# Index logits of a sparse attention: the matmuls of two heads issued in turn, lower and upper rows, into two sets of banks

## The chip, the cores and the metric

The kernel runs on one core of one Trainium2 chip. The metric is the device time of one execution in microseconds; below it is the median of three executions. The profile is of one further execution.

## What is computed

Two residual blocks run over one sequence of 512 tokens with 1024 channels. The second ends in a layer whose sparse attention first scores every key for every query. With 8 index heads of 64 channels, for a block of 128 queries:

```python
logits = jnp.einsum('bqhd,bkd->bqhk', qi, k_idx_f)
score = jnp.einsum('bqh,bqhk->bqk', wi, jax.nn.relu(logits))
score = jnp.where(s_pos[None, None, :] <= t_pos[None, :, None], score, -jnp.inf)
_, idx = lax.top_k(score, topk)
```

`qi` are 8 heads of queries, `k_idx_f` one set of keys for all heads, `wi` one weight per token and head. All three come out of one projection of the normed input (`idx_in` in the kernel). The keys chosen here are then attended to, together with a dilated local attention.

## The kernel before

All engines run programs written out by hand and meet through semaphores. The weights come as 302 chunks of 128x1024 through SyncE's queue; GpSimd splits each into a high and a low part, and TensorE multiplies both with the input (`three`, L406 to L408, and `token_body`, L433 to L435). This fills most of the time. GpSimd may be four chunks ahead of TensorE.

The phases of the last layer, in TensorE's order: `idx_in` (6 chunks: query heads in pairs, keys twice, the latent row), 24 matmuls for the head weights `wi` (L742, profiled under L406 to L408 with output `mix`), the index logits (L745 to L770), four tiny matmuls that sum the squares of the latent row (L775), then `attn_in` (16 chunks), the latent queries (L797), and the attention (`scores` L816, `turn` L827).

The queries of heads h and h+1 lie in one tile, `T2[:, h // 2, :]`: the even head in rows 0 to 63, the odd one in rows 64 to 127. `T2[:, 4, :]` holds the keys, twice. So a logits matmul contracts over 64 rows, the lower or the upper half. A head has four of them, for the four query blocks j, with 128 (j+1) keys each, in float32; each appears twice in the trace, as two passes with a weight load each: 8 passes per head, 64 in all. Even heads write banks 0 to 2 of the set `G` (called `gemm`), odd heads those of `M` (called `mix`).

For head h ScalarE waits for `ix_mm` and applies relu to the three banks into `Z[:, h % 2]` (L1695 to L1697, tile `b_z`), which raises `ix_relu`. VectorE multiplies it with the head's weight and adds it to `b_score` in four instructions (L1320 for head 0, L1322 for the rest), which raises `ix_add`. ScalarE's relu of head h waits for `ix_add` of head h-2, since `Z` has two buffers. TensorE's head h waits for the relu of head h-2, which frees its banks:

```python
if h >= 2:
    pe.wait_ge(sig("ix_relu"), h - 1)
```

Head 0 stands ahead of four small transposes of `wi` (L767), which wait for ScalarE's copy of the row (L1687); head 1 stands behind them and waits for ScalarE's second copy (L1689, `wi_ready`), which VectorE waits for too. After head 7, TensorE waits for the eighth relu before L775, as its output is in bank `M[2]`.

Of the kernel before, what the change touches and what calls it, by code (L numbers as in the profile page):

```python
# [33 lines left out]
P = 128  # L34
D = 1024
T = 512
KT = D // P
NTB = T // P
# [29 lines left out]
N0, G0 = {}, {}  # L68
# [17 lines left out]
BANK_J = [(1, 384), (2, 0), (1, 0), (0, 0)]  # L86
# [73 lines left out]
def build(nc, x_in, wstream, adastream, c_in, cols_in, const_in, mask_in, gatew_in, wiw_in, wuk_in, wuv_in, out):  # L160
    with ExitStack() as ctx:
        def sem(name):
            return ctx.enter_context(nc.semaphore(name))

        def sb(name, shape, dt=F32, where=ctx):
            return where.enter_context(nc.sbuf_tensor(name, shape, dt))
# [21 lines left out]
        G = [ctx.enter_context(nc.psum_tensor(f"gemm{i}", [P, T], F32)) for i in range(4)]  # L188
        M = [ctx.enter_context(nc.psum_tensor(f"mix{i}", [P, T], F32)) for i in range(4)]
# [3 lines left out]
        def const(name, n=128, rows=P):  # L193
            return cst[0:rows, CST[name]:CST[name] + n]
# [51 lines left out]
        with ExitStack() as r:  # L246
# [4 lines left out]
            T2 = sb("b_t2", [P, 18, T], F32, r)  # L251
# [36 lines left out]
        gfree = [sem(f"gemm_free{i}") for i in range(4)]  # L288
# [20 lines left out]
        def sig(name):  # L309

            if name not in S:
                S[name] = sem(name)
            return S[name]
# [90 lines left out]
        def _(pe):  # L404
            def three(out_ap, w_h, w_l, r_h, r_l, first, last):
                pe.matmul(out_ap, w_h, r_h, start=first, stop=False)  # L406
                pe.matmul(out_ap, w_h, r_l, start=False, stop=False)  # L407
                return pe.matmul(out_ap, w_l, r_h, start=False, stop=last)  # L408
# [191 lines left out]
            for h in range(4):  # L600
# [3 lines left out]
                o = M[h]  # L604
# [4 lines left out]
                for i in range(NTB):  # L609
                    mm = pe.matmul(o[:, i * P:(i + 1) * P], v[i], AD[:, h, i * P:(i + 1) * P], start=False, stop=(i == 3), skip_group_check=(i < 3))  # L610
                mm.then_inc(sig("hgrn_o"), 1)
            for h in range(4):
# [4 lines left out]
                for j in range(NTB):  # L617
                    mm = pe.matmul(M[0][:, 4 * h + j:4 * h + j + 1], sqt[:, h % 2, j * P:(j + 1) * P], const("ones")[:, 0:1], start=True, stop=True)
                mm.then_inc(sig("hgrn_ss"), 1)
            stick_r(0)  # L620
            for h in range(4):
                pe.wait_ge(sig("hgrn_diag"), h + 1)
                for j in range(NTB):
                    mm = pe.matmul(M[h][:, j * P:(j + 1) * P], const("ones"), work[:, h, j * P:(j + 1) * P], start=True, stop=True)
# [18 lines left out]
            for k in range(KT):  # L643
                w = slice(GW * k, GW * k + GW)
                mm = three(M[2][0:GW, :], gw_hi[:, w], gw_lo[:, w], Hhi[:, k, :], Hlo[:, k, :], k == 0, k == KT - 1)
# [6 lines left out]
            for j in range(NTB):  # L652
                mm = pe.transpose(M[0][:, 8 * j:8 * j + 8], GA[:, j * P:(j + 1) * P], const("ident")[0:8, 0:8])
# [86 lines left out]
            for k in range(KT):  # L740
                w = slice(8 * k, 8 * k + 8)
                mm = three(M[0][0:8, :], wi_hi[:, w], wi_lo[:, w], Hhi[:, k, :], Hlo[:, k, :], k == 0, k == KT - 1)  # L742
            mm.then_inc(sig("wi_mm"), 1)

            def index_logits(h):  # L745
                rows = slice(64 * (h % 2), 64 * (h % 2) + 64)
                bk = M if h % 2 else G
                if h == 0:
                    for u in range(4):
                        pe.wait_ge(gfree[u], G0["attn_in"][u])  # L750
                if h == 1:
                    pe.wait_ge(sig("wi_ready"), 1)
                    pe.wait_ge(sig("x_normed"), KT)
                if h >= 2:

                    pe.wait_ge(sig("ix_relu"), h - 1)
                for j in range(NTB):
                    b, o = BANK_J[j]
                    mm = pe.matmul(bk[b][:, o:o + P * (j + 1)], T2[rows, h // 2, j * P:(j + 1) * P], T2[rows, 4, 0:P * (j + 1)],
                                   start=True, stop=True)  # L760
                mm.then_inc(sig("ix_mm"), 1)

            index_logits(0)

            pe.wait_ge(sig("wi_rows"), 1)
            for j in range(NTB):
                mm = pe.transpose(M[3][:, 8 * j:8 * j + 8], wirow[:, j * P:(j + 1) * P], const("ident")[0:8, 0:8])  # L767
            mm.then_inc(sig("wi_t"), 1)
            for h in range(1, 8):
                index_logits(h)  # L770

            pe.wait_ge(sig("ckv_sq"), 1)
            pe.wait_ge(sig("ix_relu"), 8)
            for j in range(NTB):
                mm = pe.matmul(normps[:, j:j + 1], sqt[:, 0, j * P:(j + 1) * P], const("ones")[:, 0:1], start=True, stop=True)  # L775
# [8 lines left out]
            for j in range(NTB):  # L784
                mm = pe.transpose(M[1][:, j * P:(j + 1) * P], T2[:, 5, j * P:(j + 1) * P], const("ident"))
            mm.then_inc(sig("ckv_t"), 1)

            for h in range(8):
                rows = slice(64 * (h % 2), 64 * (h % 2) + 64)
# [1069 lines left out]
```

## Time and profile before

| what | value |
|---|---|
| median of 3 executions | 2149.22 us (2148.58 to 2151.42) |
| profiled execution | 2155.03 us, its span 2153.0 us |
| mean granted TensorE clock in it | 0.964 |
| stretch of the index logits, first logits matmul to L775 | 1478.76 to 1497.40 us |

The span runs from the first to the last instruction of the program. Times in rows are microseconds from the span's start; PE is TensorE's matmuls, PEld its weight loads, ACT ScalarE, DVE VectorE, POOL GpSimd, SP SyncE. A matmul's duration has its way through the array in it, so matmuls that follow one another overlap in their records.

### The profile page before, as it was taken

What the parts mean: (1) busy time and instruction counts of PE and PEld (TensorE: products, weight loads), DVE (VectorE), ACT (ScalarE), POOL (GpSimd) and SP (SyncE); (2) the same over time, 40 slices, a digit from 0 to 9 for tenths busy, and PEclk for the clock granted to TensorE, in tenths of its full rate; (3) what the DMA queues carried; (4) which work ended last, traced back from release to release, by engine and by line L of the source; (5) the groups of instructions that cost most, each with busy time, mean ns of one, the idle gap of its engine ahead of it and who ended that gap; (6) DMA issues with size and microseconds to landing.
All of it is one profiled execution on the core that took longest, in us unless ns stands there. A gap on an engine that the chain in (4) does not pass through costs nothing.

```text
span 2153.0 us, 25278 instructions
## 1 busy us (share of the span) xinstructions
PE 2020.8 (94%) x8706; PEld 1593.8 (74%) x8706; DVE 1063.0 (49%) x1623; ACT 440.4 (20%) x778; POOL 1185.8 (55%) x907
## 2 busy tenths in 40 slices
PE   3998788999999989999999999999989899999998
PEld 2777665888888877854888888876855478888886
DVE  5566633766664454056666653243666544333222
ACT  3300143211110023122221111022125412111100
POOL 2774401587778846610587877753640055666673
PEclk8998888999999999988999999999989999999999
DMA  7532200355555622300255543321220022222332
GB/s 279 186 137 98 98 1 10 115 207 193 195 185 207 214 99 91 97 30 0 98 184 193 189 146 107 99 97 59 88 69 1 1 69 88 93 95 95 101 105 77
DMA packets 67609, 242.07 MB, mean 112 GB/s; under 512 B 7768, under 2 KB 8152, under 8 KB 67552
## 3 DMA queue, kind: packets, MB, share of 16 engines
q1 hardware_dynamic: 65520, 236.18, 32.2%
q10 hardware_dynamic: 2032, 5.10, 0.7%
q8 instruction: 39, 0.64, 0.1%
q14 instruction: 18, 0.15, 0.0%
HBM read 239.15 MB, written 2.10 MB: 112 GB/s over the span
## 4 chain that ended last, share of the span: by engine, by line
PE 59%; issue 16%; POOL 14%; DMA 6%; ACT 3%; DVE 3%; POOLq 0%; SPq 0%; DVEq 0%; ACTq 0%
PE gemm L406 16%; PE gemm L408 15%; PE gemm L407 15%; POOL w_lo L390 7%; DMA w_raw<-wstream 5%; POOL w_hi L388 5%; POOL pool_gate L387 2%; PE mix L816 1%; ACT b_z L1722 1%; PE gemm L674 1%; PE gemm L433 1%; PE gemm L688 1%; PE gemm L435 1%; PE gemm L434 1%; PE mix L488 1%
## 5 line engine op out<-in xcount | busy, mean ns | idle before, releaser
L390 POOL TENSOR_TENSOR w_lo<-w_raw,w_hi 128x1024 fp32r<-128x1024 f32 x302 | 742.4, 2458 | 25.1
L406 PE MATMUL gemm<-h_hi,w_hi 128*128 128x512 f32 x1680 | 660.0, 393 | 19.2 <-DVE h_lo L994 11.0
L407 PE MATMUL gemm<-h_lo,w_hi 128*128 128x512 f32 x1680 | 657.2, 391 | 0.0
L408 PE MATMUL gemm<-h_hi,w_lo 128*128 128x512 f32 x1680 | 657.2, 391 | 0.0
L387 POOL TENSOR_TENSOR pool_gate<-pool_gate 128x1 f32<-128x1 f32 x298 | 111.7, 375 | 889.9 <-PE gemm L408 828.7
L406 PEld LDWEIGHTS gemm<-h_hi,w_hi 128*128 128x128 f32 x1680 | 317.8, 189 | 91.3 <-issue 25.4
L408 PEld LDWEIGHTS gemm<-h_hi,w_lo 128*128 128x128 f32 x1680 | 317.5, 189 | 66.9
L407 PEld LDWEIGHTS gemm<-h_lo,w_hi 128*128 128x128 f32 x1680 | 317.8, 189 | 66.4 <-issue 0.5
L388 POOL TENSOR_SCALAR w_hi<-w_raw 128x1024 fp32r<-128x1024 f32 x302 | 344.2, 1140 | 22.3 <-DMA w_raw<-wstream 22.3
L881 DVE CUSTOM_DVE_ANT_0 ada_raw<-ada_raw,c_act 128x1024 f32<-128x1024 f32 x128 | 209.1, 1637 | 202.6 <-DMA ada_raw<-adastream 202.6
L408 PE MATMUL gemm<-p_hi,w_lo 128*128 128x512 f32 x528 | 205.4, 389 | 0.0
L406 PE MATMUL gemm<-p_hi,w_hi 128*128 128x512 f32 x528 | 205.4, 389 | 0.0
L407 PE MATMUL gemm<-p_lo,w_hi 128*128 128x512 f32 x528 | 205.4, 389 | 0.0
L899 DVE SCALAR_TENSOR_TENSOR x_res<-gemm,modv,x_res 128x512 f32<-128x512 f32 x48 | 35.8, 747 | 203.7 <-PE gemm L408 203.7
L1164 DVE TENSOR_TENSOR work<-work,gemm 128x512 f32<-128x512 f32 x66 | 45.4, 688 | 184.2 <-PE gemm L408 150.4
L1166 DVE TENSOR_TENSOR p_lo<-work,p_hi 128x512 f32 x66 | 104.7, 1587 | 61.4 <-ACT p_hi L1590 61.4
L1427 ACT ACTIVATE sq_tile<-x_res 128x512 f32 (+1 forms) x56 | 35.3, 632 | 464.4 <-DVE x_res L899 451.9
L1136 DVE TENSOR_TENSOR sq_acc<-sq_acc,sq_tile 128x512 f32<-128x512 f32 x42 | 99.6, 2372 | 36.7 <-ACT sq_tile L1427 36.7
L407 PEld LDWEIGHTS gemm<-p_lo,w_hi 128*128 128x128 f32 x528 | 99.1, 188 | 20.7
L406 PEld LDWEIGHTS gemm<-p_hi,w_hi 128*128 128x128 f32 x528 | 99.1, 188 | 20.6
L408 PEld LDWEIGHTS gemm<-p_hi,w_lo 128*128 128x128 f32 x528 | 99.1, 188 | 20.4
L1584 ACT ACTIVATE work<-work 128x512 f32<-128x512 f32 x44 | 27.8, 632 | 283.3 <-DVE work L1159 283.3
(288 smaller groups left out, 1979.2 us busy)
## 6 DMA issues: line engine op xcount, KB each, us to landing
w_raw<-wstream SPq DMA_DIRECT2D x302, 512.0 KB, 3.4
ada_raw<-adastream SPq DMA_DIRECT2D x128, 512.0 KB, 4.2
a_early<-adastream SPq DMA_DIRECT2D x16, 512.0 KB, 15.3
x_res<-x_in ACTq DMA_DIRECT2D x4, 512.0 KB, 10.0
out<-x_res SPq DMA_DIRECT2D x8, 256.0 KB, 2.2
c_act<-c_in ACTq DMA_DIRECT2D x2, 512.0 KB, 16.1
b_dist<-const_in ACTq DMA_DIRECT2D x1, 512.0 KB
cst<-const_in ACTq DMA_DIRECT2D x1, 448.0 KB, 4.5
```

The lines of the kernel that those rows point to most:

```text
L387: pool.tensor_tensor(pgate[:], pgate[:], pgate[:], ALU.mult)
L388: pool.tensor_scalar(whi[s][:], raw[:, u % RAW, :], 1.0, 0.0, ALU.mult, ALU.add).then_inc(w_hi_done, 1)
L390: pool.tensor_tensor(wlo[s][:], raw[:, u % RAW, :], whi[s][:].bitcast(F32), ALU.subtract).then_inc(w_split, 1)
L406: pe.matmul(out_ap, w_h, r_h, start=first, stop=False)
L407: pe.matmul(out_ap, w_h, r_l, start=False, stop=False)
L408: return pe.matmul(out_ap, w_l, r_h, start=False, stop=last)
L881: dve.tensor_tensor_reduce(w, w, c, 1.0, start, ALU.mult, ALU.add, total).then_inc(ada_used, 1)
L899: dve.scalar_tensor_tensor(out=X[:, ds(m, 1), :].rearrange("p a t -> p (a t)"), in0=G[bank][:], scalar=modv[:, ds(gate + m, 1)], in1=X[:, ...
L1136: dve.tensor_tensor(sqacc[:], sqacc[:], sqt[:, m % 2, :], ALU.add).then_inc(sq_added, 1)
L1164: dve.tensor_tensor(work[:, 2 + jj, :], y, G[2 * jj + 1][:], ALU.mult).then_inc(gfree[2 * jj + 1], 1)
L1166: dve.tensor_tensor(Plo[:, ds(2 * i + jj, 1), :].rearrange("p a t -> p (a t)"), work[:, 2 + jj, :], Phi[:, ds(2 * i + jj, 1), :].rearrange ...
L1427: act.activation(sqt[:, slot, :], X[:, ds(m, 1), :].rearrange("p a t -> p (a t)"), ACT.Square).then_inc(sq_ready, 1)
```

## The change

TensorE's program changes, no other. The transposes of `wi` now stand ahead of all logits. Then four pairs of heads follow. In a pair the four query blocks are walked once, and for each the even head's matmul (lower rows, set `G`) and the odd head's (upper rows, set `M`) are issued one behind the other. A pair waits for the relu of both heads of the pair before it. `ix_mm` is raised by the last matmul of each head. The wait for `wi_ready` is gone from TensorE. The number and the shapes of the matmuls, the transposes and all work of the other engines are as before.

```diff
-            def index_logits(h):
-                rows = slice(64 * (h % 2), 64 * (h % 2) + 64)
-                bk = M if h % 2 else G
-                if h == 0:
-                    for u in range(4):
-                        pe.wait_ge(gfree[u], G0["attn_in"][u])
-                if h == 1:
-                    pe.wait_ge(sig("wi_ready"), 1)
-                    pe.wait_ge(sig("x_normed"), KT)
-                if h >= 2:
-
-                    pe.wait_ge(sig("ix_relu"), h - 1)
-                for j in range(NTB):
-                    b, o = BANK_J[j]
-                    mm = pe.matmul(bk[b][:, o:o + P * (j + 1)], T2[rows, h // 2, j * P:(j + 1) * P], T2[rows, 4, 0:P * (j + 1)],
-                                   start=True, stop=True)
-                mm.then_inc(sig("ix_mm"), 1)
-
-            index_logits(0)
-
             pe.wait_ge(sig("wi_rows"), 1)
             for j in range(NTB):
                 mm = pe.transpose(M[3][:, 8 * j:8 * j + 8], wirow[:, j * P:(j + 1) * P], const("ident")[0:8, 0:8])
             mm.then_inc(sig("wi_t"), 1)
-            for h in range(1, 8):
-                index_logits(h)
+
+            def index_pair(p):
+                if p == 0:
+                    for u in range(4):
+                        pe.wait_ge(gfree[u], G0["attn_in"][u])
+                    pe.wait_ge(sig("x_normed"), KT)
+                else:
+                    pe.wait_ge(sig("ix_relu"), 2 * p)
+                for j in range(NTB):
+                    b, o = BANK_J[j]
+                    for h, bk in ((2 * p, G), (2 * p + 1, M)):
+                        rows = slice(64 * (h % 2), 64 * (h % 2) + 64)
+                        mm = pe.matmul(bk[b][:, o:o + P * (j + 1)], T2[rows, p, j * P:(j + 1) * P], T2[rows, 4, 0:P * (j + 1)],
+                                       start=True, stop=True)
+                        if j == NTB - 1:
+                            mm.then_inc(sig("ix_mm"), 1)
+
+            for p in range(4):
+                index_pair(p)
```

## Rows read from the trace of the kernel before

**Rows 1.** The page: span, TensorE's busy time, chain that ended last by engine.

```profile
span 2153.0 us, 25278 instructions
PE 2020.8 (94%) x8706; PEld 1593.8 (74%) x8706; DVE 1063.0 (49%) x1623; ACT 440.4 (20%) x778; POOL 1185.8 (55%) x907
...
PE 59%; issue 16%; POOL 14%; DMA 6%; ACT 3%; DVE 3%; POOLq 0%; SPq 0%; DVEq 0%; ACTq 0%
```

**Rows 2.** The chain that ended last, logits and after: start us, us, what.

```profile
1489.23 0.28 ACT b_z L1697
1489.56 1.97 PE mix L759 x7
...
1497.40 1.48 PE mix L775 x8
...
1500.38 0.43 PE gemm L406
...
1505.15 0.23 PE gemm L406
```

**Rows 3.** Timeline, start of the stretch: start us, us, engine, line, [idle before].

```profile
1478.76 2.42 PE L759 MATMUL gemm<-b_t 64*128 64x128 f32 x8
1478.87 0.59 ACT L1687 ACTIVATE b_ol<-mix 8x512 f32<-8x512 f32 x1 [4.21 <-PE mix L408]
...
1481.12 0.41 PE L767 MATMUL mix<-cst,b_ol 8*128 8x8 f32 x4
```

**Rows 4.** Timeline, heads 1 (mix) and 2 (gemm).

```profile
1481.81 1.56 PE L759 MATMUL mix<-b_t 64*128 64x128 f32 x6 [0.29 <-ACT b_wi L1689]
...
1483.07 0.37 PE L759 MATMUL gemm<-b_t 64*128 64x128 f32 x1
...
1483.22 0.59 PE L759 MATMUL mix<-b_t 64*128 64x512 f32 x1
...
1483.65 0.59 PE L759 MATMUL mix<-b_t 64*128 64x512 f32 x1
...
1484.27 0.60 ACT L1695 ACTIVATE b_z<-mix 128x512 f32<-128x512 f32 x1 [1.26 <-PE mix L759]
...
1485.53 0.60 ACT L1695 ACTIVATE b_z<-gemm 128x512 f32<-128x512 f32 x1
1485.67 14.19 DVE L1322 SCALAR_TENSOR_TENSOR b_score<-b_z,b_wi,b_score 128x128 f32<-128x128 f32 x28 [1.28 <-ACT b_z L1697]
...
1486.50 0.39 ACT L1697 ACTIVATE b_z<-gemm 128x256 f32<-128x256 f32 x1
```

**Rows 5.** Timeline, latent queries: four heads, lower and upper rows in turn.

```profile
1591.91 1.99 PE L797 MATMUL gemm<-b_t,b_wuk 64*128 64x512 f32 x8 [1.81 <-ACT b_va L1707]
```

**Rows 6.** Windows: start:end us, length, busy by engine, granted clock, DMA.

```profile
1487.98:1491.86 3.88, 3.68 (x17) 2.31 (x15) 3.67 (x9) 2.72 (x6) 0.00 (x0) 1.00 0.02 4
...
1495.90:1497.40 1.50, 0.00 (x0) 0.03 (x1) 1.50 (x4) 1.36 (x3) 0.00 (x0) 1.00 0.00 0
...
1497.80:1504.60 6.80, 6.80 (x20) 5.54 (x20) 3.64 (x11) 0.27 (x1) 0.00 (x0) 0.50 0.00 0
```

**Rows 7.** Windows in the first block's mixer, same columns.

```profile
333.00:345.00 12.00, 8.75 (x25) 5.29 (x24) 3.40 (x12) 3.64 (x7) 0.00 (x0) 0.72 0.00 0
345.00:362.00 17.00, 12.41 (x42) 8.92 (x41) 6.30 (x13) 7.46 (x14) 0.00 (x0) 0.80 0.00 0
```

**Rows 8.** Attention: one window, then its timeline at either clock.

```profile
1600.20:1620.70 20.50, 14.65 (x31) 7.26 (x30) 9.87 (x40) 6.07 (x20) 0.00 (x0) 0.50 0.00 1
...
1602.94 4.63 PE L816 MATMUL mix<-b_t 64*128 64x128 f32 x8 [1.83 <-DVE b_mx L1375]
...
1623.10 2.42 PE L816 MATMUL mix<-b_t 64*128 64x128 f32 x8
```

**Rows 9.** Waits behind the stretch: who waited for whom, us in total, times, longest.

```profile
POOL pool_gate L387 <- PE gemm L408: 50.4, 12, 30.2
...
DVE b_t L1336 <- PE mix L514: 22.9, 1, 22.9
```

## Prediction

> **What bounds the kernel now.** I read the page first. TensorE has matmuls in flight for 2020.8 of 2153.0 us, and the chain that ended last is 59% TensorE [rows 1]. So time lost on TensorE is lost at the end unless it sits in a stage that something else bounds. The change touches one stage, from 1478.76 to 1497.40 us. There I read the chain, then the timeline, then who waits behind it.
>
> In this stage the chain alternates: matmuls of one head (L759), relu of the same head on ScalarE (L1695 to L1697), matmuls of the head two further on [rows 2]. The banks are what is scarce: each set of three is filled, emptied, and only then filled again. The reader should see in the timeline that two such cycles run shifted against each other. While ScalarE empties the even set, TensorE fills the odd one. Head 1 starts at 1481.81 and head 5, two turns later on the same set, at 1489.56 [rows 4, 2]: a turn of 3.88 us in which two heads are done. TensorE is busy for 3.68 us of such a turn [rows 6], and VectorE needs 14.19 us for the 28 additions of seven heads, 2.03 per head or 4.05 per two [rows 4]. VectorE, TensorE and the cycle of the banks are all near 4 us per two heads.
>
> **Do the two row halves run together at all?** This is the point of the change, and the trace of before answers it twice. Head 2 (lower rows) starts at 1483.07, while the last two passes of head 1 (upper rows) still start at 1483.22 and 1483.65. The relus, which wait for the real ends, begin at 1484.27 and 1485.53 [rows 4]: each head takes 2.46 us from its first matmul to its relu, as if it had the array alone, though 1.2 us of it is shared. And the latent queries issue heads in just the order of the change, two passes on the lower rows, then two on the upper. Their first eight 512-column passes take 1.99 us [rows 5]. Passes of one half follow each other 0.43 us apart [rows 4], so eight in a line would need about 3.5 us. So a pair of logits heads should take 2.46 us instead of twice that. The halves already overlap for a part in the kernel before; only the rest is new.
>
> **The change, part by part.**
>
> *The transposes ahead of the logits.* ScalarE's copy of the row ends at 1478.87 + 0.59 = 1479.46 [rows 3]. TensorE follows a ScalarE end after 0.05 us (1489.23 + 0.28 to 1489.56) [rows 2], and the four transposes take 0.41 us [rows 3]. The first pair starts at 1479.92 instead of 1478.76: 1.16 us later. Before, head 0 covered this wait; now nothing does. The removed wait for the weights' second copy had held head 1, which now starts with head 0; that is in the sum below. VectorE still needs that copy, but its first relu now comes at 1479.92 + 2.46 + 1.36 = 1483.74, long after. The wait for the normed input had been met before the stage.
>
> *The turn of a pair.* A pair waits for both relus of the pair before it, and both of its heads need the banks that these empty. So filling and emptying no longer overlap; what is issued together is also waited for together. A turn is: matmuls to relu 2.46, two relus back to back 1484.27 to 1486.50 + 0.39 = 1486.89, that is 2.62 [rows 4], and 0.05 to the next pair. Sum 5.13 us per two heads against 3.88. That is above the 4.05 of VectorE, so VectorE doesn't bind and its waits for `Z` are met. Four turns are 20.52 us, and L775 would start at 1479.92 + 20.52 = 1500.44 instead of 1497.40 [rows 2]: **3.0 us later** with the clock at its full level.
>
> A rule of the Trainium skill (TensorEngine Tiling, PSUM Bottleneck) speaks against this change too: tiling speeds up the matmuls but not the emptying of the banks, which may become the limit. In this trace the two relus, 2.62 us, are the larger part of the new turn; no other sum comes out of it.
>
> *The clock.* Here I have to choose. Before, the granted clock is 1.00 through the stage. Then TensorE has nothing for 1.5 us, runs the tiny L775, and from 1497.80 to 1504.60 the clock is 0.50, its 1.2 GHz level [rows 6]. After the change each turn has 2.67 us of its 5.13 without a matmul: nearly half, four times over. In the mixer of the first block, where TensorE also works in bursts and is busy for 73% of the time, the mean clock is 0.72 and 0.80 [rows 7], which is half the time or 40% of it at the lower level. I expect the clock to fall inside the stage. The price per pair at the lower level is that of a head of `scores`, which has the same eight passes: 4.63 against 2.42 us [rows 8], 2.2 more. Bounds: no pair (0) to all four (8.8 us). I take two, by the half of the time in the mixer: **4.4 us**.
>
> *Behind the stage.* After L775 the lower clock costs matmuls of 0.43 instead of 0.23 us [rows 2] over 5.85 us, about 14 of them, 2.8 us. I expect such a stretch again, so nothing changes; it can vanish or double, 2.8 us to either side. VectorE ends its additions some 3.4 us later, but the first join behind it, the broadcast into L1336, made it wait 22.9 us [rows 9], and that moves with TensorE. GpSimd had its four chunks ready and waited 30.2 us for TensorE [rows 9]; so does SyncE's queue behind it. Nobody catches the delay up.
>
> **Sum.** 3.0 + 4.4 = 7.4 us. The profiled execution would take 2155.03 + 7.4 = 2162.4 us. It lies 5.8 us above the median of the runs shown; against that median the forecast is 2149.22 + 7.4 = **2156.6 us**, 0.34% slower.
>
> **Rivals.**
>
> *The clock holds.* Both halves at work make the bursts denser, and the pauses are each under 3 us. Then only 3.0 us remain: 2152.2, within 0.2%. For it: in the stage before, half of the array alone kept the clock. Against: the fall after a pause of 1.5 us [rows 6].
>
> *Passes in strict order.* The upper half's first pass starts only with the second of the lower half, and the other way round at each step. Then each turn has one 512-column pass more, 0.43 us, 1.7 in all: 2158.3. The row against it is head 2 starting ahead of head 1's last passes [rows 4].
>
> The Trainium skill (TensorE: Matmul & The Clock Gate, Part 3) states that matmuls keep program order in start and in end. By it the sum would be that of this rival, 2158.3 us; the starts in this trace differ from it.
>
> *The halves don't overlap when interleaved.* Then both heads of a pair are done only after twice the passes, 2.2 us more per turn, 8.8 in all, without any fall of the clock: 2161.0. The latent queries speak against it.
>
> *Faster, by the clock.* The later arrival shifts what comes after against the chip's changes of clock. In the attention the clock is 0.50 from 1600.20 to 1620.70 [rows 8]; there VectorE waits for TensorE, and two heads of scores at 2.2 us each are in it. If that stretch and the one at 1497.80 (2.8) both go, because denser bursts keep the clock up, 7.2 us come back against 3.0 lost: 2145.0, just on the other side of 0.2%. It decides only if the clock holds in the stage as well. Nothing in the rows asks for it.
>
> **How the numbers follow.** What a measurement of this kernel can tell from no change is about 0.2%, 4.3 us, so 2144.9 to 2153.5. Chances: the forecast, with one to three slow pairs, 62%, nearly all of it slower (one slow pair alone gives 2154.4); the clock holds 15%, within; strict order 9%, slower; no overlap 5%, slower; faster by the clock 5%; the rest, a delay swallowed somewhere that I don't see, 4%, within. With a little spread over the bound: slower 0.73, same 0.20, faster 0.07. The range takes in the clock that holds and the case of four slow pairs (2161.0), and leaves out the faster case: 2151.0 to 2161.0.
>
> **What would show it.** In the changed profile the two sets' passes should start within about 0.1 us of each other, and a pair at full clock last 2.4 to 2.5 us. The relus should stand in blocks of 2.6 us with no matmul beside them, and L759's wait for L1697 should be near 2.7 us, three times. The first pair should start at 1479.9, and turns be 5.1 us, or 7.3 where the clock is low. The windows should show a clock under 1.00 between 1480 and 1500. I am wrong if the turns are nearer 4 us, if L775 starts before 1500, or if a later stage takes the delay back.

## The result, and the profile after

The changed kernel takes 2160.12 us (median of 6, 2158.47 to 2167.4) against 2152.19 us of the kernel before, run beside it: a ratio of 1.0044, 95% interval 1.0030 to 1.0058, or 9.5 us slower (6.5 to 12.5). The ratio is taken over all executions; the two medians alone lie 7.9 us apart. The forecast was slower by 7.4 us. Its range ended at 2161.0 us; the ratio applied to 2152.19 gives 2161.7, just above it, while the median itself, 2160.12, lies inside.

The timeline of the changed kernel, first pair and the start of the second (L761 is a pair's matmuls; relus are now L1692 to L1694, VectorE's additions L1317 and L1319, the squares of the latent row L772):

```profile
1475.74 0.37 PE L761 MATMUL gemm<-b_t 64*128 64x128 f32 x1
1475.75 0.37 PE L761 MATMUL mix<-b_t 64*128 64x128 f32 x1
...
1477.58 0.59 PE L761 MATMUL gemm<-b_t 64*128 64x512 f32 x1
1477.58 0.59 PE L761 MATMUL mix<-b_t 64*128 64x512 f32 x1
1478.20 0.60 ACT L1692 ACTIVATE b_z<-gemm 128x512 f32<-128x512 f32 x1 [2.15 <-PE mix L761]
...
1480.39 0.43 ACT L1694 ACTIVATE b_z<-mix 128x256 f32<-128x256 f32 x1
...
1480.87 0.48 PE L761 MATMUL gemm<-b_t 64*128 64x128 f32 x1 [2.70 <-ACT b_z L1694]
...
1485.02 0.60 ACT L1692 ACTIVATE b_z<-gemm 128x512 f32<-128x512 f32 x1 [4.20 <-PE mix L761]
...
1487.69 0.48 PE L761 MATMUL gemm<-b_t 64*128 64x128 f32 x1 [2.70 <-ACT b_z L1694]
...
1501.41 1.77 PE L772 MATMUL mix<-cst,sq_tile 128*128 128x1 f32 x8 [2.79 <-ACT b_z L1694]
```

Both halves start within 0.01 us of each other at each of the eight passes, and the first pair takes 2.46 us to its relu (1475.74 to 1478.20), as one head did [rows 4]. The change does what it says. But TensorE then stands idle for 2.70 us while ScalarE empties both sets. The first turn is 5.13 us (1475.74 to 1480.87), the second 6.82 (1480.87 to 1487.69): its matmuls take 4.15 us to the relu (1480.87 to 1485.02).

The windows of the same stretch show why; the last column but two is the granted clock:

```profile
1480.80:1484.20 3.40, 3.33 (x14) 2.23 (x16) 2.08 (x5) 0.02 (x1) 0.00 (x0) 0.53 0.00 0
1484.20:1487.60 3.40, 0.79 (x4) 0.00 (x0) 1.19 (x3) 2.58 (x6) 0.00 (x0) 0.97 0.00 0
1487.60:1491.00 3.40, 3.31 (x14) 2.21 (x16) 2.69 (x6) 0.04 (x1) 0.00 (x0) 0.53 0.00 0
1491.00:1494.40 3.40, 0.80 (x4) 0.00 (x0) 1.17 (x3) 2.57 (x6) 0.00 (x0) 0.96 0.00 0
1494.40:1497.90 3.50, 3.40 (x14) 2.21 (x16) 2.71 (x6) 0.05 (x1) 0.00 (x0) 0.54 0.02 5
1497.90:1501.30 3.40, 0.72 (x4) 0.00 (x0) 1.26 (x4) 2.62 (x6) 0.00 (x0) 0.97 0.00 0
1501.30:1508.10 6.80, 6.69 (x20) 5.66 (x21) 4.31 (x12) 0.27 (x1) 0.00 (x0) 0.51 0.00 0
```

The clock is at its 1.2 GHz level while the matmuls of pairs two to four run and at 2.4 GHz while TensorE waits. It falls only as a pair begins (the 64x128 passes take 0.48 and 0.42 us in the second pair, 0.37 and 0.27 in the first), and is up again before the pair's last pass ends (0.63 us for that 64x512 pass, 1.05 for the one before it). So the pauses run at the full level and the work between them at the lower. Three of the four pairs are hit. Whether the pauses are the cause is tested in e4.

Who waited for whom in this stretch (us in total, times, longest):

```profile
ACT b_z L1692 <- PE mix L761: 14.7, 4, 4.2
...
PE gemm L761 <- ACT b_z L1694: 8.1, 3, 2.7
...
PE mix L772 <- ACT b_z L1694: 2.8, 1, 2.8
```

TensorE waits for ScalarE 8.1 + 2.8 us and ScalarE for TensorE 14.7 us. In the kernel before each worked beside the other, and the same waits were 0.4 + 1.5 us and 4.1 us:

```profile
ACT b_z L1695 <- PE mix L759: 4.1, 4, 1.3
...
PE mix L775 <- ACT b_z L1697: 1.5, 1, 1.5
...
PE mix L759 <- ACT b_z L1697: 0.4, 2, 0.2
```

Two windows serve as the measure for all kernels below: A, from the last matmul of the head weights to the first of `attn_in`, and B, from there to the start of the 301st matmul, until the clock behind the stage no longer differs. First before, then after:

```profile
1478.44:1498.75 20.31, 18.09 (x79) 11.41 (x77) 13.73 (x31) 11.47 (x26) 0.00 (x0) 0.98 0.07 24
1498.75:1570.01 71.26, 71.26 (x302) 58.41 (x303) 43.66 (x129) 7.44 (x13) 41.52 (x36) 0.96 0.25 81
```

```profile
1474.34:1503.04 28.70, 17.13 (x78) 9.93 (x77) 13.86 (x31) 11.26 (x26) 0.00 (x0) 0.79 0.05 17
1503.04:1574.03 70.99, 70.99 (x301) 58.19 (x302) 43.54 (x129) 7.46 (x13) 41.67 (x36) 0.96 0.25 81
```

A + B is 91.6 us before and 99.7 after: 8.1 us lost there. The spans differ by only 3.5 us (2153.0 and 2156.5), because the profiled execution of before was 4 us behind when it came to this stage; stages that the change doesn't touch differ by that much from one execution to the next.

### The profile page after: what moved, and what is told of

It is laid out like the page before. It is cut to its first block, busy times and chain, and to the rows that moved or that the text cites. A ratio compares the mean times of both kernels' runs of the same rounds, so it can differ in the third digit from the quotient of the medians.

```text
span 2156.5 us, 25277 instructions
## 1 busy us (share of the span) xinstructions
PE 2015.8 (93%) x8706; PEld 1588.8 (74%) x8706; DVE 1070.5 (50%) x1623; ACT 440.3 (20%) x778; POOL 1195.9 (55%) x907
## 4 chain that ended last, share of the span: by engine, by line
PE 59%; issue 16%; POOL 14%; DMA 6%; ACT 3%; DVE 3%; POOLq 0%; SPq 0%; DVEq 0%; ACTq 0%
PE gemm L406 15%; PE gemm L408 15%; PE gemm L407 15%; POOL w_lo L390 7%; DMA w_raw<-wstream 5%; POOL w_hi L388 5%; POOL pool_gate L387 2%; ACT b_z L1719 1%; PE mix L813 1%; PE gemm L688 1%; PE gemm L674 1%; PE gemm L433 1%; PE gemm L435 1%; PE gemm L434 1%; PE mix L488 1%
## 5 line engine op out<-in xcount | busy, mean ns | idle before, releaser
L387 POOL TENSOR_TENSOR pool_gate<-pool_gate 128x1 f32<-128x1 f32 x298 | 116.4, 391 | 883.2 <-PE gemm L408 822.7
L406 PEld LDWEIGHTS gemm<-h_hi,w_hi 128*128 128x128 f32 x1680 | 317.6, 189 | 91.4 <-issue 25.3
```

The lines of the kernel that those rows point to most:

```text
L387: pool.tensor_tensor(pgate[:], pgate[:], pgate[:], ALU.mult)
```

## The experiments

Each kernel was run in turn with the kernel before on the same chip: 5 executions each of e1 and e3, 11 of e2, e4, e5, e6 and e10, 12 of e7, against 15 to 29 of before. e5, e6 and e7 ran on a second chip, the other experiments on a first. An interval of a ratio is 2 to 3 us to either side.

**e1: the changed kernel again.**

> The changed kernel once more, to compare the others with on one chip. Theory (bank waits plus clock): slower than before by 0.35 to 0.55%, first logits matmul to the squares of the latent row (L772) 25 to 28 us, of which 20.5 are four turns at full clock and 1.7 more for each pair that meets the lower clock. Rival (the loss sits elsewhere, in chance changes of the clock ahead of the stage): the ratio moves towards 1.001 in a second sample.

Ratio 1.0045 (1.0031 to 1.0059). A is 28.61 us, B 71.13. From the first logits matmul to L772 it takes 25.7 us here (1476.54 to 1502.23) as in the profile shown above (1475.74 to 1501.41), with turns of 5.13, 6.83, 6.82 and 6.91 us. The loss is no chance of the first sample.

**e2: the transposes alone.** From the kernel before:

```diff
-            index_logits(0)
             pe.wait_ge(sig("wi_rows"), 1)
             ...
             mm.then_inc(sig("wi_t"), 1)
-            for h in range(1, 8):
+            for h in range(8):
                 index_logits(h)
```

The wait of head 1 for `wi_ready` is gone too.

> The kernel before with one part of the change: the transposes of the head weights ahead of all logits, heads still one after the other, each waiting for the relu two heads before. Theory: heads 0 and 1 now start nearly together, VectorE's additions run through with about 4.05 us per two heads, and the stage lasts 17 to 18 us plus 1.1 us of late start: within 0.1% of before (-1 to +1 us). Rival (the transposes' place costs): 1.1 us or more of the loss, 0.05% or more slower.

Ratio 1.0000 (0.9990 to 1.0009), A 19.68 us. By themselves the moved transposes cost nothing: heads 0 and 1 now start 0.76 us apart (1476.65 and 1477.41), the stage to the squares is 17.4 us in place of 18.6, and that pays for the later start.

**e3: the pair's wait, but heads in a row.** From the changed kernel:

```diff
-                for j in range(NTB):
-                    b, o = BANK_J[j]
-                    for h, bk in ((2 * p, G), (2 * p + 1, M)):
+                for h, bk in ((2 * p, G), (2 * p + 1, M)):
+                    for j in range(NTB):
+                        b, o = BANK_J[j]
```

> The changed kernel with its waits per pair, but in a pair the whole lower head is issued first, then the whole upper head. Theory (the wait for both relus costs, the order of issue hardly matters): the upper head starts 1 to 2 us after the lower, while the lower is emptied, so the second relu is hardly late; a turn of 5.1 to 5.6 us at full clock, the whole 0.3 to 0.55% slower than before. Rival (the order of issue is what costs or gains): in a row the pair takes 4.3 us or more, a turn 5.9 us or more, at least 3 us slower than the changed kernel; or, if issuing in turn is itself the loss, back to the time of before.

Ratio 1.0046 (1.0032 to 1.0060). The first pair in its timeline:

```profile
1474.44 1.24 PE L761 MATMUL gemm<-b_t 64*128 64x128 f32 x5
...
1475.20 0.48 PE L761 MATMUL mix<-b_t 64*128 64x128 f32 x2
...
1475.52 0.48 PE L761 MATMUL gemm<-b_t 64*128 64x384 f32 x1
...
1476.90 0.60 ACT L1692 ACTIVATE b_z<-gemm 128x512 f32<-128x512 f32 x1 [2.15 <-PE gemm L761]
...
1478.13 0.62 ACT L1692 ACTIVATE b_z<-mix 128x512 f32<-128x512 f32 x1
...
1479.57 2.26 PE L761 MATMUL gemm<-b_t 64*128 64x128 f32 x5 [1.95 <-ACT b_z L1694]
```

Issued eight and eight, the upper half starts 0.76 us after the lower, ahead of the lower head's last three passes, and the turn at full clock is 5.13 us (1474.44 to 1479.57): the same to 0.01 us as issued in turn. So at full clock the order of issue is not what costs, and it buys nothing either, since the second relu is queued behind the first. The upper head started earlier than the 1 to 2 us I had expected. At the lower clock the row order is worse (its later turns are 7.5 us: 1479.57, 1487.08, 1494.60), and over the next three pairs and their pauses the clock did not come up:

```profile
1479.60:1500.10 20.50, 17.60 (x48) 10.91 (x48) 9.74 (x21) 6.28 (x14) 0.00 (x0) 0.50 0.00 0
```

Its A is 29.89 us, 1.2 more than the changed kernel's; its B, 70.15, is 0.8 less.

**e4: the pauses filled.** From the changed kernel:

```diff
+            def fill(n):
+                for _ in range(n):
+                    pe.matmul(G[3][:, 0:256], const("ones"), cst[:, 0:256], start=True, stop=True)
             for p in range(4):
                 index_pair(p)
+                fill(5)
```

> The changed kernel with five matmuls of 128x256 float32 into an unused bank behind each pair, so that TensorE is at work in the pauses; their output is never read. Theory (the pauses make the clock fall): clock 1.00 through the stage, four turns of 5.1 to 5.3 us, L772 20.5 to 21.3 us after the first pair, and no stretch at 0.50 behind L772; against the changed kernel 5 us back in the stage and up to 2.8 behind it, so 0.0 to 0.2% slower than before. Rival (the clock falls for another reason, such as both row halves at work at once): the clock still falls and the time stays 0.35% or more above before.

Ratio 1.0003 (0.9994 to 1.0012). Its turns and its two windows:

```profile
1480.69 0.37 PE L761 MATMUL gemm<-b_t 64*128 64x128 f32 x1 [0.35 <-ACT b_z L1699]
...
1485.82 0.37 PE L761 MATMUL gemm<-b_t 64*128 64x128 f32 x1 [0.34 <-ACT b_z L1699]
...
1490.95 0.37 PE L761 MATMUL gemm<-b_t 64*128 64x128 f32 x1 [0.35 <-ACT b_z L1699]
...
1496.17 1.02 PE L777 MATMUL mix<-cst,sq_tile 128*128 128x1 f32 x8 [0.44 <-ACT b_z L1699]
```

```profile
1474.15:1497.06 22.91, 20.76 (x119) 13.71 (x117) 13.12 (x29) 11.26 (x26) 0.00 (x0) 1.00 0.06 21
1497.06:1565.59 68.53, 68.53 (x303) 56.40 (x303) 44.28 (x132) 7.44 (x13) 41.55 (x36) 1.00 0.26 85
```

With useless work in the pauses the clock is 1.00 throughout, and the first three turns are 5.13 us each (the first pair starts at 1475.56), as the prediction's sum at full clock had them; the fourth, to the squares, is 5.22. A is 5.8 us shorter than in the changed kernel, B 2.5. The clock is what takes most of the loss, and the pauses are what takes the clock. The rival of this run, that two halves at work bring it down, has fallen: they work together here too.

**e5: the kernel before, its one pause filled.** Four of the same matmuls ahead of `pe.wait_ge(sig("ckv_sq"), 1)`.

> The kernel before with four matmuls of 128x256 float32 into an unused bank between head 7 and the squares of the latent row; their output is never read. Theory (a pause ahead of the tiny matmuls makes the clock fall, and the stretch behind it costs): logits stage as long as before (18.6 us), no stretch at 0.50 behind it, 2.8 us back, 0.1 to 0.15% faster than before. Rival (the pause is not the cause): the stretch at 0.50 is there again and the time is the same.

Ratio 0.9995 (0.9986 to 1.0003), which is no clear gain. In the trace the theory holds:

```profile
1477.73:1497.72 19.99, 19.31 (x87) 12.47 (x85) 13.41 (x30) 11.47 (x26) 0.00 (x0) 1.00 0.06 23
1497.72:1566.28 68.56, 68.56 (x302) 56.39 (x302) 43.99 (x130) 7.46 (x13) 41.64 (x36) 1.00 0.26 85
```

No lower clock is left, although the same tiny matmuls run, and A + B is 3.0 us less than in the first profile of before. That the run shows only 1.1 us of it, less than the 0.1 to 0.15% expected, is taken up under e8.

e4 and e5 are the changed kernel and the kernel before with the clock at 1.00 throughout. Side by side they show what the order and the waits cost without the clock: A + B 91.4 against 88.5 us, 2.9 us, where the prediction's sum had 3.0.

**e6 and e10: the squares moved out of the end of the stage.** From e2; ScalarE reads `M[3][:, 64:68]` in place of `normps`:

```diff
+            pe.wait_ge(sig("ckv_sq"), 1)
+            for j in range(NTB):
+                mm = pe.matmul(M[3][:, 64 + j:65 + j], sqt[:, 0, j * P:(j + 1) * P], const("ones")[:, 0:1], start=True, stop=True)
+            mm.then_inc(norm_sum, 1)
             pe.wait_ge(sig("wi_rows"), 1)
...
-            pe.wait_ge(sig("ckv_sq"), 1)
-            pe.wait_ge(sig("ix_relu"), 8)
-            ...
-            mm.then_inc(norm_sum, 1)
+            pe.wait_ge(sig("ix_relu"), 7)
```

> Heads one after the other with the wait of two heads before, transposes ahead, and the squares of the latent row moved ahead of the transposes into bank M[3], so that attn_in waits only for the relu of head 6. Theory (the turn of the banks overlaps and nothing is left at the end of the stage): the squares are partly hidden by ScalarE's copy of the row and add 0.3 to 0.6 us, attn_in starts 0.2 us after head 7's last pass, no fall of the clock behind it: about 3 us from the tail and 2.8 from the clock, 0.2 to 0.3% faster than before. Rival (attn_in is held by something else, or the clock falls anyway): within 0.1% of before.

> e6 once more, for a narrower interval. In its profile the stretch is 85.7 us, 5.9 less than in the first profile of before. Theory (before is 1 to 3 us shorter there on average): 0.15 to 0.25% faster than before, stretch 85.7 us again as no stretch of lower clock stands in it. Rival (the gain of the stage is lost elsewhere): 0.0 to 0.1% faster.

Ratios 0.9990 (0.9981 to 0.9998) and, run again on the first chip, 0.9979 (0.9970 to 0.9988). The first missed the 0.2 to 0.3% expected, the second is in its range. This beats both kernels, by 0.1 to 0.2% of before. The profile of e10:

```profile
1476.31:1493.44 17.13, 16.01 (x79) 10.59 (x77) 10.86 (x24) 10.11 (x23) 0.00 (x0) 1.00 0.07 27
1493.44:1561.97 68.53, 68.53 (x301) 56.40 (x302) 46.55 (x136) 8.72 (x16) 41.69 (x36) 1.00 0.26 84
```

The eighth relu and the squares no longer stand between the logits and `attn_in`, and with the pause went the fall of the clock.

**e7: pairs, pauses filled, squares early.** The changed kernel with e4's filling behind the first three pairs and e6's squares.

> Pairs as in the changed kernel, pauses filled behind the first three pairs, squares early as in e6. Theory (with the clock held, the pair's wait costs 5.13 against some 4.0 us per two heads, and nothing else separates the two orders): attn_in starts 2 to 4 us later, counted from the last matmul of the head weights, than in e6, so slower than e6 by 0.1 to 0.2% and 0.0 to 0.15% faster than before. Rival (the pairs cost nothing once the clock is held): as fast as e6.

Ratio 1.0002 (0.9992 to 1.0013), A 20.90 us and B 68.54. Against e6 A is 3.8 us longer at the same clock of 1.00: as the order of issue is worth nothing at that clock (e3), this is the pair's wait by itself. In time I had expected 0.1 to 0.2% more than e6; it is 0.12% against e6 and 0.23% against e10. Against before I had expected 0.0 to 0.15% less; the interval reaches from 0.08% less to 0.13% more.

**e8 and e9: the kernel before, two more profiles.** One execution each.

> The kernel before, profiled once more. From the last matmul of the head weights to the 300th matmul after attn_in's first it took 91.6 us in the first profile; all seven other kernels came out 0.7 to 3.7 us slower against before than this stretch of theirs says. Theory: the first profile of before caught a long stretch of lower clock behind the squares (6.8 us, 2.8 us dear), others catch a shorter one or none, so 88.5 to 90.5 us here. Rival (the difference comes from stages ahead of or behind this one): 91.6 us again.

> The same kernel a third time, for the same question: theory 88.5 to 90.5 us for that stretch, rival 91.6 us again.

The windows A and B, and the stretch of lower clock, of e8:

```profile
1475.74:1495.58 19.84, 17.62 (x78) 10.95 (x77) 13.27 (x30) 11.47 (x26) 0.00 (x0) 1.00 0.06 24
1495.58:1565.76 70.18, 70.18 (x303) 57.58 (x302) 44.13 (x130) 7.44 (x13) 41.51 (x36) 0.98 0.26 82
1496.00:1499.40 3.40, 3.40 (x10) 2.65 (x9) 2.84 (x8) 0.02 (x1) 0.00 (x0) 0.50 0.00 0
```

A + B is 90.0 us, and 19.84 + 70.14 = 90.0 in e9 as well, with a lower clock for 3.4 us in place of 6.8 [rows 6]. The first profile of before was 1.6 us dearer than these two. Set against 90.0 us, the sums A + B come close to the ratios, each times 2151 us (A + B is one profile of a kernel, the ratio a mean of many executions):

| kernel | A + B, us | against 90.0 | by the ratio |
|---|---|---|---|
| changed | 99.7 | +9.7 | +9.5 |
| e1 | 99.7 | +9.7 | +9.7 |
| e2 | 89.8 | -0.2 | 0.0 |
| e3 | 100.0 | +10.0 | +9.9 |
| e4 | 91.4 | +1.4 | +0.6 |
| e5 | 88.5 | -1.5 | -1.1 |
| e6, e10 | 85.7 | -4.3 | -2.2, -4.5 |
| e7 | 89.4 | -0.6 | +0.4 |

All but e6's first sample agree within 1 us, which is closer than the intervals can tell, and that one lies outside by 0.2 us even at the end of its interval (-4.1). What took it there stays open; the second sample, on the first chip, doesn't show it. The three samples of the second chip, e5 to e7, lie 0.4 to 2.1 us above their windows; no profile shows the A + B of before on that chip. Three profiles don't say how often before gets the long stretch.

## Why the prediction was right or wrong

**Overlap of the row halves: right.** 2.46 us for a pair, taken from [rows 4, 5], is what the first pair took. Passes in strict order (0.43 us more per turn) and no overlap (2.2 more) both fell. The prediction took matmuls that start in program order to mean passes in strict order, and that step fell with it: in the changed kernel the two halves start in program order (1475.74, then 1475.75), and no pass is lost.

**Later start of the first pair: right in size.** From the last matmul of the head weights it is 1475.74 - 1474.34 = 1.40 us against 0.32, so 1.1 later, as forecast. In the order of before the same late start costs nothing (e2), since head 1 no longer waits for the transposes; in pairs it is part of the 3.0.

**The turn: right.** Forecast 5.13 us at full clock; measured 5.13 in the changed kernel's first turn, in e3's first and in e4's first three. The 3.0 us for the whole stage at full clock stand against 2.9 between e4 and e5.

**The clock: the mechanism right, the size off.** "I take two" pairs at 2.2 us each, 4.4 us, was the term that was mis-sized. Three pairs were hit in both profiles of the changed kernel, at 1.7 us each (6.82 against 5.13), because the clock falls only as a pair begins and comes up again before its last pass is through. That is 5.1 us. The choice of two rested on the mixer; a nearer row, the attention's heads with the same eight passes, had the clock at 0.50 for all of 20.5 us with TensorE busy for 71% of it [rows 8], and was read only for the price. Two errors cancel in part: fewer pairs than were hit, at more than each cost.

**Behind the stage: the step of the slowdown that failed.** "I expect such a stretch again, so nothing changes" put at nothing what measured 1.6 us. It took the 6.8 us of lower clock in the one profile of before as usual. In e8 and e9 it is 3.4 us; with the changed kernel it was 6.8 both times (B 70.99 and 71.13 against 70.18 and 70.14), and the squares themselves run at the lower clock now (L772, 1.77 and 1.66 us in its two profiles, against 1.48 in [rows 2] and 1.02 in e4, e8 and e9). Together these are the 1.6 us. Why the stretch is the longer one in both profiles of the changed kernel stays open: before had it once in three, and e2 and e3 have the shorter. The sum in the runs' own terms, against e8 and e9: start 1.1, turns 20.5 in place of 18.6 (1.9), slow pairs 5.1, squares and the step to `attn_in` 0.7, behind the stage 0.9, in all 9.7, against 9.5 and 9.7 by the ratios. The two misses, 0.7 and 1.6 us, point the same way. By time alone they could not be told: the interval of the slowdown, 6.5 to 12.5 us, takes in the forecast 7.4. The windows show them.

**The base: what put the time outside the range.** The prediction's sum, "against that median the forecast is 2149.22 + 7.4", added the slowdown to the median of three executions of before. Run beside the changed kernel the median of before was 2152.19 us, 3.0 us more, and 2151.4, 2151.2 and 2152.1 in the later, larger samples. That the base was low is the larger part of the miss of 5.1 us (2156.6 to 2161.7), the 2.1 us of slowdown the smaller. As a slowdown the range was 1.8 to 11.8 us, its upper end four slow pairs or no overlap of the halves, and 9.5 us lies well inside; 2149.22 times the ratio is 2158.7. The prediction saw that the profiled execution lay 5.8 us above its base and did not widen the range for it.

**Nobody catches the delay up: right.** The broadcast's wait (now L1333) is 22.7 us against 22.9, so VectorE moved with TensorE, and GpSimd's longest wait for TensorE behind the stretch is 38.3 us against 30.2: longer by the 8.1 us that A + B grew between the two profiles. e1 to e7 show at the end about what A + B shows, e6's first sample excepted.

## What to carry to other kernels

Two buffers overlap only while each is waited for alone: issuing two users together and waiting for both turns double buffering into fill, empty, fill, whatever the issue order gains. Here the order gained nothing at full clock, since the two row halves had overlapped without it; the wait alone cost 3.8 us (e7 against e6). Before a regrouping, look which pauses it puts on TensorE: here pauses of 2.7 us were paid a second time in clock, with more (5.1 us in the stage) than the lost overlap itself. Take more than one profile of the kernel before, if the sum rests on a stretch of lower clock, and more than three executions, if a time and not a ratio is forecast to within some microseconds.

## What the runs showed of the hardware

TensorE's two row halves don't keep one order. In e3 the upper half's first pass starts while three passes of the lower half, issued before it, have not begun. The Trainium skill (TensorE: Matmul & The Clock Gate, Part 3) says that matmuls are in program order in start and in end; the starts in e3 and in [rows 4] are not. The order of the ends, on which a single semaphore at the end of a group relies, is not shown by these records.

A pause of 1.54 us ahead of the squares went with a lower clock for 3.4 us (e8, e9) or 6.8 [rows 6]; with useless matmuls in it, and the squares as before, the clock stayed at 1.00 (e5).

The clock rose within one pair of half-array matmuls issued in turn, both halves at work at once (0.53 from 1480.80 to 1484.20, then 0.97), but stayed at 0.50 for 20.5 us over three pairs issued in a row (e3), where the halves overlap for a part only. Passes, shapes and waits are the same in both; their first turns are equal and at full clock. Whether the alternation helps the clock by itself or by where its bursts fell in time was not tried.
